# Position bias tables of the sparse attention made at the program's start, one row per head, through a DRAM table

## What is computed

```
def rel_bucket(dist):
    n = jnp.maximum(dist, 0)
    ...
    return jnp.where(n < max_exact, n, large)
...
    table = rel_bias.astype(f32).reshape(REL_BUCKETS, G, HPG).transpose(1, 2, 0)
...
        lc = (jnp.einsum('bghqd,bgkd->bghqk', qc, k_cmp).astype(f32) * scale
              + table[:, :, rel_bucket(tq[:, None] - cmp_end[None, :])])
...
        lw = (jnp.einsum('bghqd,bgkd->bghqk', qc, kw).astype(f32) * scale
              + table[:, :, rel_bucket(dist)])
```

## Time and profile before

| | before |
|---|---|
| median of 3 runs | 1943.29 us (1943.08 to 1943.59) |
| profiled execution | 1943.08 us, span 1941.3 us |
| TensorE busy | 1815.1 us (94%), mean granted clock 0.959 |
| VectorE, ScalarE, GpSimd busy | 595.7, 358.9, 217.7 us |
| the chain that ended last | TensorE 84%, VectorE 8%, issue 3%, DMA 2% |

### The profile page before, as it was taken

How to read it: one execution, slowest core, us unless ns; L and a number is a source line. 1 busy time by engine, 2 the same in 40 slices (tenths; PEclk the granted TensorE clock), 3 DMA queues, 4 the chain that set the end, 5 groups by cost and what they waited for, 6 DMA issues and landing times.

```text
span 1941.3 us, 25898 instructions
## 1 busy us (share of the span) xinstructions
PE 1815.1 (94%) x11066; PEld 959.5 (49%) x11066; DVE 595.7 (31%) x1273; ACT 358.9 (18%) x842; POOL 217.7 (11%) x263
## 2 busy tenths in 40 slices
PE   7979988989799999999969998999979999999993
PEld 3334347755554454445444576555554444454440
DVE  5463793452221111111040434564122111111113
ACT  1442113311100000000030113665110000000001
POOL 1044000000000000000020001454000000000002
PEclk9989998999799999999969999999979999999997
DMA  5111743060899999999969202010379999999994
GB/s 206 52 78 42 278 123 52 3 268 1 345 414 430 428 427 432 430 428 429 418 233 155 62 22 109 13 30 5 130 289 407 427 432 428 431 427 430 429 402 151
DMA packets 60930, 499.73 MB, mean 257 GB/s; under 512 B 28079, under 2 KB 28591, under 8 KB 42383
## 3 DMA queue, kind: packets, MB, share of 16 engines
q1 hardware_dynamic: 53391, 481.26, 62.1%
q0 software_dynamic: 7424, 16.80, 2.4%
HBM read 465.23 MB, written 41.18 MB: 261 GB/s over the span
## 4 chain that ended last, share of the span: by engine, by line
PE 84%; DVE 8%; issue 3%; DMA 2%; POOL 1%; ACT 1%; SPq 0%; POOLq 0%; DVEq 0%
PE bank L1397 71%; PE bank L1449 5%; PE bank L1985 3%; PE bank L1999 2%; DVE spare L1008 2%; DVE arena L1009 1%; PE bank L1785 1%; DVE arena L1260 1%; DMA arena<-y_rows,ints 1%; POOL arena L493 1%; DMA arena<-gram_dram 1%; PE bank L1405 1%; POOL arena L491 0%; DVE arena L1022 0%; PE bank L1557 0%
## 5 line engine op out<-in xcount | busy, mean ns | idle before, releaser
L1397 PE MATMUL bank<-arena 128*64 128x512 f32 (+10 forms) x5202 | 1258.8, 540 | 25.3 <-DVE arena L973 9.5
L1397 PEld LDWEIGHTS bank<-arena 128*64 128x64 f32 (+5 forms) x5202 | 485.2, 156 | 675.9 <-issue 653.0
L1397 PEld LDWEIGHTS bank<-const,arena 128*128 128x128 f32 x2048 | 238.2, 195 | 51.2 <-issue 48.7
L1397 PE MATMUL bank<-const,arena 128*128 128x128 f32 x2048 | 250.0, 281 | 2.2 <-DVE const L1139 2.2
L513 POOL DMA_INDIRECT y_rows<-arena,ints x64 | 63.0, 985 | 1124.3 <-ACT arena L749 909.5
L1214 DVE TENSOR_TENSOR arena<-arena,bank 128x256 f32<-128x256 f32 x64 | 26.9, 421 | 426.5 <-ACT arena L743 426.5
L749 ACT ACTIVATE arena<-bank 128x512 f32<-128x512 f32 x64 | 38.2, 597 | 424.3 <-PE bank L1397 424.3
L743 ACT ACTIVATE arena<-bank 128x256 f32<-128x256 f32 x64 | 24.5, 383 | 468.6 <-PE bank L1397 468.6
L1146 DVE TENSOR_TENSOR arena<-bank,vec 128x512 f32<-128x512 f32 x64 | 44.3, 691 | 192.7 <-PE bank L1397 192.7
L559 POOL TENSOR_SCALAR arena<-arena,small 128x128 f32<-128x128 f32 (+3 forms) x128 | 76.5, 607 | 150.6 <-DVE small L1374 150.6
L1223 DVE COPY arena<-bank 128x256 f32<-128x256 f32 x64 | 27.1, 424 | 184.3 <-PE bank L1785 184.3
(11 more groups left out here) (238 smaller groups left out, 980.7 us busy)
## 6 DMA issues: line engine op xcount, KB each, us to landing
arena<-m_w SPq DMA_DIRECT2D x64, 4096.0 KB, 18.5
arena<-m_w SPq DMA_DIRECT2D x64, 2048.0 KB, 16.5
y_rows<-state SPq DMA_DIRECT2D x1, 8192.0 KB, 22.6
arena<-kv_w SPq DMA_DIRECT2D x1, 6144.0 KB, 18.3
rev_bias<-arena SPq DMA_DIRECT2D x1, 5120.0 KB, 69.7
arena<-a_wk SPq DMA_DIRECT2D x2, 2048.0 KB, 14.9
arena<-a_wr SPq DMA_DIRECT2D x2, 2048.0 KB, 7.9
arena<-a_wv SPq DMA_DIRECT2D x2, 2048.0 KB, 8.0
```

The source lines that it names most:

```text
L1397: return nc.tensor.matmul(dst, lhsT, rhs, start=start, stop=stop)
```

## The change

It does four things.

- The one-hot matrices and the bias values are loaded once, by ScalarE's own DMA instructions, as its first three instructions. Four products (three of 16x512, one of 16x128) are the first on TensorE. VectorE copies their results into `bias_rows` (16 rows of 1664) ahead of its first normalization step; SP writes them to DRAM behind the first weight loads.
- The columns of `bucket_fwd` are permuted on the way in, so that `bias_c` is eight DMA reads of that DRAM table (rows of 55 values), issued behind the load of `w_kv`.
- `rev_dram` is filled from the DRAM table instead of from SBUF, without a wait of its own.
- The 57 products, the four copies and the six loads at the end of the first mixture of experts go. Several semaphore names share counters in a new way; that moves no instruction.

```diff
+            sp.wait_ge(sem("bias_ev"), 4)
+            sp.dma_start(bias_dram, bias_rows).then_inc(sem("bias_out"), 16)
             sp.wait_ge(sem("tr_done"), NK)
...
             sp.wait_ge(sem("expert_mm"), at("expert_mm", E - 2))
-            for i in range(2):
-                sp.dma_start(fwd[i], d["bucket_fwd"]).then_inc(sem("bias_in"), 16)
-                sp.dma_start(rev[i], d["bucket_rev"]).then_inc(sem("bias_in"), 16)
-                sp.dma_start(rel[i][0:32, :], d["rel_bias"]).then_inc(sem("bias_in"), 16)
...
             sp.dma_start(w_kv, d["kv_w"]).then_inc(sem("kv_w_in"), 16)
+            for a in range(8):
+                sp.dma_start(bias_c[16 * a:16 * a + 16, :, :],
+                             bass.AP(tensor=bias_dram.tensor, offset=9 - a, ap=[[64, 16], [1664, NH], [1, NOFF]])
+                             ).then_inc(sem("bias_c_in"), 16)
...
-            sp.wait_ge(sem("rev_ev"), at("rev_ev", 1))
-            sp.dma_start(rev_dram, spread(rev_rows, 1, P)).then_inc(sem("rev_out"), 16)
+            sp.dma_start(rev_dram, spread(bias_dram[:, 1024:1664], 1, P)).then_inc(sem("rev_out"), 16)
...
+            nc.scalar.dma_start(fwd, d["bucket_fwd"]).then_inc(sem("bucket_in"), 16)
+            nc.scalar.dma_start(rev, d["bucket_rev"]).then_inc(sem("bucket_in"), 16)
+            nc.scalar.dma_start(rel[0:32, :], d["rel_bias"]).then_inc(sem("bucket_in"), 16)
             act.wait_ge(sem("gn_eps"), 1)
...
+            act.wait_ge(sem("bias_out"), 16)
             for m in range(4):
                 k_squares(m)
...
-            act.wait_ge(sem("bias_mm"), at("bias_mm", 1))
-            nc.scalar.activation(rev_rows[:, 0:512], bank[2][0:NH, :], ACT.Copy, scale=-1.0)
-            nc.scalar.activation(rev_rows[:, 512:640], bank[3][0:NH, 0:128], ACT.Copy, scale=-1.0)
...
+            nc.vector.memset(rel[32:33, :], NEG).then_inc(sem("rel_mask"), 1)
+            dve.wait_ge(sem("bias_mm"), 1)
+            for i in range(2):
+                nc.vector.tensor_copy(bias_rows[:, 512 * i:512 * i + 512], bank[4 + i][0:NH, :]).then_inc(sem("bias_ev"), 1)
+            nc.vector.tensor_scalar(bias_rows[:, 1024:1536], bank[6][0:NH, :], -1.0, None, ALU.mult).then_inc(sem("bias_ev"), 1)
+            nc.vector.tensor_scalar(bias_rows[:, 1536:1664], bank[7][0:NH, 0:128], -1.0, None, ALU.mult).then_inc(sem("bias_ev"), 1)
             for j in range(NJ + 1):
...
+            dve.wait_ge(sem("bias_c_in"), at("bias_c_in", 128))
             then(nc.vector.tensor_scalar(cmask, bias_c[:, 0, :], 0.1 * NEG, None, ALU.is_gt))
...
+            pe.wait_ge(sem("bucket_in"), 48)
+            pe.wait_ge(sem("rel_mask"), 1)
+            for i in range(2):
+                mm(bank[4 + i][0:NH, :], rel, fwd[:, 512 * i:512 * i + 512])
+            mm(bank[6][0:NH, :], rel, rev[:, 0:512])
+            mm(bank[7][0:NH, 0:128], rel, rev[:, 512:640]).then_inc(sem("bias_mm"), 1)
...
-            for m in range(NOFF):
-                mm(bank[m % 2][:, 16 * (m // 2):16 * (m // 2) + 16], fwd[m % 2][:, 864 - 16 * m:992 - 16 * m], rel[m % 2])
-            mm(bank[3][0:NH, 0:128], rel[1], rev[1][:, 512:640])
-            mm(bank[2][0:NH, :], rel[0], rev[0][:, 0:512]).then_inc(sem("bias_mm"), 1)
-            pe.wait_ge(sem("rev_ev"), at("rev_ev", 1))
```

More of the change, by code:

```diff
@@ L63 @@
     "gates_ready": ("l_ready", 8), "xTkv_act": ("d_ready", 8), "xTkv_dve": ("e_ready", 8),
-    "router_mm": ("ae_ready", 8), "place_mm": ("r_ready", 8), "b_wo_mm": ("kt_ready", 8), "bias_mm": ("rk_ready", 8),
-    "rel_mask": ("gd_act", 8), "rev_ev": ("gd_masked", 8), "group_shifted": ("lora_mm", 8), "group_exp": ("gd_mm", 8),
+    "router_mm": ("ae_ready", 8), "place_mm": ("r_ready", 8), "b_wo_mm": ("kt_ready", 8),
+    "store_rows": ("rel_mask", 1), "table_zero": ("bias_mm", 1), "table_clear": ("bias_out", 16),
+    "gram_out": ("bucket_in", 48), "tri_in": ("ident_in", 16), "router_in": ("vec_in", 16), "y_clear": ("const_in", 16),
+    "group_shifted": ("lora_mm", 8), "group_exp": ("gd_mm", 8),
     "top_diff": ("g_mm", 8), "top_exp": ("g_ev", 8), "two_hot": ("v_ev", 8), "h_nsa": ("l_kept", 8), "cmp_zero": ("rn_mm", 8),
@@ L268, in decoder_program @@
         bias_c = spare[:, 0:NH * NOFF].rearrange("p (h m) -> p h m", h=NH)
[L269 to L272, removed]
+        fwd, rev, rel = (region(11)[0:33, a:b] for a, b in ((0, 1024), (1024, 1664), (1664, 1680)))
+        bias_rows = region(11)[0:NH, 2048:3712]
+        bias_dram = nc.dram_tensor("bias_rows", (NH, 1664), FP32, kind="Internal").ap()
         xT_b = region(6).rearrange("p (k t) -> p k t", k=NK)
@@ L336, in _ @@
             sp.dma_start(half_w[1], d["a_wv"][1]).then_inc(sem("half_in1"), 16)
-            sp.wait_ge(sem("gram_out"), 256)
+            sp.wait_ge(sem("gram_out"), at("gram_out", 256))
             sp.dma_start(tri, gram_dram).then_inc(sem("tri_in"), 16)
@@ L367, in _ @@
             sp.dma_start(router_b, d["router_b"].rearrange("l p n -> p l n")).then_inc(sem("router_in"), 16)
-            sp.wait_ge(sem("table_zero"), 1)
+            sp.wait_ge(sem("table_zero"), at("table_zero", 1))
             for l in range(2):
@@ L506, in moe_pool @@
             def moe_pool(l):
-                pool.wait_ge(sem("y_clear"), 32)
-                pool.wait_ge(sem("store_rows"), l + 1)
+                pool.wait_ge(sem("y_clear"), at("y_clear", 32))
+                pool.wait_ge(sem("store_rows"), at("store_rows", l + 1))
                 for e in range(E):
@@ L520, in moe_pool @@
                 with pool.If(n_over > 0):
-                    pool.wait_ge(sem("table_clear"), 32)
+                    pool.wait_ge(sem("table_clear"), at("table_clear", 32))
                     for j in range(NJ):
@@ L986, in _ @@
             ring_mix(2, 3)
-            dve.wait_ge(sem("tri_in"), 16)
+            dve.wait_ge(sem("tri_in"), at("tri_in", 16))
             flat = tri.rearrange("p s t -> p (s t)")
@@ L1049, in _ @@
                     if c == 0:
-                        dve.wait_ge(sem("y_clear"), 32)
+                        dve.wait_ge(sem("y_clear"), at("y_clear", 32))
                     for par in range(2):
@@ L1411, in _ @@
                 for k in range(NK):
+                    if j == 0 and k >= 4:
+                        pe.wait_ge(sem("bias_ev"), k - 3)
                     last = nc.tensor.transpose(bank[k][:, P * j:P * j + P], xn[:, j, P * k:P * k + P], ident)
@@ L1743, in moe_pe @@
                 projected(6)
-                pe.wait_ge(sem("router_in"), 32)
+                pe.wait_ge(sem("router_in"), at("router_in", 32))
                 pe.wait_ge(sem(added), at(added, 6))
@@ L2114 @@
     x["consts"], x["bucket_rev"], x["bucket_fwd"] = shape_constants()
+    at = np.arange(1024)
+    x["bucket_fwd"] = x["bucket_fwd"][:, 16 * (63 - at % 64) + at // 64]
     nc = bacc.Bacc("TRN2", target_bir_lowering=False, num_devices=1, dynamic_dma_scratch_size=8192)
```

10 lines of the change are left out of this document (1 added, 9 removed), and 2 rows, old and new, of the table GOES_ON.

## The result

The changed kernel takes 1948.28 us (median of 22 executions, 1943.26 to 1960.95) where the kernel before takes 1942.99 us (22 executions, 1937.57 to 1950.63). The ratio is 1.0032 [1.0022, 1.0043]: slower by 0.32%, and the interval lies wholly above 1. The medians alone are 5.3 us apart (a ratio of 1.0027), and the ratio of 1.0032 stands for 6.2 us. In 4 of the 22 executions of the kernel before and 3 of the 22 of the changed one, the time is 6 to 13 us longer than the median. The profiled execution took 1949.12 us and its span grew from 1941.3 to 1947.2 us, 5.9 us.

The account below looks back on a forecast made before the run. TensorE was busy 94%, but the start's chain of waits was taken to decide: landing 5.0, start 0.1, products 5.2, copies 2.35, step 0.15 put root 0 +4.2 us later; removal and middle 0; 1947.5 us, range 1944.2 to 1950.5.

Parts of the forecast that it names:

- The sum as a whole: At the start, landing, products, copies and normalization step add up; root 0 moves from 8.64 to about 12.85 us, +4.2 us.
- The rival by which less is lost: At the start, earlier landing, full-clock products or warm transposes: 1943.5 to 1947.1 us, taken at 1945.5; 40%.
- Step 1, the landing: Start: ScalarE's three loads land at 5.0 us, using a small early load's 3.4 us landing; bounds 4.1 and 8.9.
- Step 2, the products: Start: four bias products on TensorE take 5.2 us, with 2.9 (full clock) and 5.8 (half clock) as ends.
- Step 3, the copies: Start: VectorE's four copies out of PSUM take 2.35 us, then the first normalization step 0.15 us.
- x's second block: Start: the new loads hold up the second block of x by 0.7 us at most, hidden behind VectorE.
- The transposes and the projection: Behind root 0: transposes start at 14.2 instead of 9.96 us, as slow as before; everything moves by 4.2 us.
- The rival "less is lost" by warm transposes: Part of the 40% rival: products lift the clock, transposes save some 1.5 of 6.3 us, giving +2.7 us.
- a projection at full clock: Part of the 40% rival: the first projection's 5.13 us at half clock run at full clock, saving another 2.6 us.
- The removal: End of first mixture of experts: the 114 removed instructions lie under the gather of the experts' rows; worth 0.
- The middle adds: Middle: eight `bias_c` reads on SP at 0.63 us each delay what follows by 5 us, but are covered; 0.
- The copy from DRAM to DRAM: Middle: as long as before, cost 0; rival at twice the time stalls the second compression MLP, +31 us, 3%.

Follow-up runs that it names:

- first experiment: Changed kernel with VectorE's wait and four copies moved behind its normalization loop and the transposes reordered; 1940.71 us, ratio 0.9989 to the kernel before.
- fourth: Changed kernel with all four products and copies 128 columns wide, most of the bias table left zero; 1943.42 us, ratio 1.0010 to the kernel before.
- fifth: Kernel before with the three new loads on ScalarE's queue at the start, unused; 1941.57 us, ratio 0.9998 to the kernel before.
- second: Kernel before with everything of the change, but done at the old place in the middle; 1943.11 us, ratio 1.0007 to the kernel before.
- third: Changed kernel with the old six loads, 57 products and four ScalarE copies put back, results unused; 1948.40 us, ratio 1.0026 to the kernel before.

## Why the prediction was right, by its own steps

**The sum as a whole.** Forecast 1947.5 us, measured 1948.28. That is nearer than the change itself was forecast: +4.2 us against 5.3 by the medians and 6.2 by the ratio, a fifth to a third too little, while the kernel before came out 0.3 us lower than the median that the forecast started from. The rival by which less is lost had 40% against the forecast's 45%. The mechanism was right: new work ahead of the first normalization step in VectorE's written order delays root 0, and the delay is carried to the end unshortened. The first, fourth and fifth experiments show it: with the work at another place the loss is gone, with a fraction of the work most of it is gone, and the loads by themselves cost nothing. The sum gave +4.2 us and root 0 moved by 5.54, so the forecast was 1.3 us too low at root 0.

**Step 1, the landing.** Forecast 5.0 us; the wait ended at 6.2 and the first product started at 6.25. Too low by 1.2 us, the largest of the three errors. ScalarE's first issue took 0.61 us, and the third went out at 1.69 as forecast; the landing took 4.52 us behind that, not the 3.4 of the row that was chosen, and 4.9 to 5.1 us in the four other runs that wait for it. The row itself did not stay what it was: the same 64 KB load took 4.7 us in the changed kernel. It took 4.5 to 5.0 us in all six runs with the three early loads and 3.4 to 3.6 in all six without them. So the added loads slow a small load beside them by about 1.2 us, which is the size of the miss, and a row of the kernel before was the wrong measure for them. The blocks of x took 5.9 us instead of 6.3. What the loads compete for was not isolated.

**Step 2, the products.** Forecast 5.2 us, with 5.8 as its upper end, and measured 5.72: too low by 0.5 us. All six wide passes took 1052 ns on average, close to the 1044 ns of a pass at half clock; the rise that the forecast let fall inside them did not come. The page's window gives them a granted clock of 1.00, as it gave, and their durations contradict it.

On this the Trainium skill, page "TensorE: Matmul & The Clock Gate", section "What's actually happening", says that the throttled state is the default and that activity ends it; the trace agrees with it by the 1052 ns and the 424 ns, and not with the window's 1.00.

**Step 3, the copies.** Forecast 2.35 us and 0.15 for the step, measured 12.01 to 14.18 us, 2.17 in all. Too high by 0.3 us: copies of one engine follow each other at 0.64 us, not at the 0.69 of a lone one.

**x's second block.** A delay of up to 0.7 us was allowed for; it arrived at 7.11 us instead of 7.58.

**The transposes and the projection.** They move with root 0 (5.55 and 5.67 us) and are as slow as before: the first 26 take 5.79 us, against 5.73 for 27. The clock fell in the gap ahead of the projection as forecast. The windows of the changed kernel at the projection's start and five microseconds on:

```profile
25.00:26.00 1.00, 0.06 (x1) 0.09 (x1) 0.96 (x3) 0.00 (x0) 0.00 (x0) 0.50 1.01 426
...
30.00:31.00 1.00, 1.00 (x2) 0.34 (x1) 0.96 (x2) 0.00 (x0) 0.00 (x0) 0.50 0.00 0
31.00:32.00 1.00, 1.00 (x3) 0.53 (x2) 0.96 (x3) 0.00 (x0) 0.00 (x0) 0.72 0.00 0
```

The half-clock stretch has moved with the work. The rival "less is lost" by warm transposes fell, since the 33-row products did not lift the clock. Its sizes were sound: transposes that wide products precede are 2.1 us shorter than in the trace of before and 1.2 shorter than in that of the loads alone (rival: 1.5), and a projection at full clock is 2.6 and 1.7 us shorter (rival: 2.6).

**The removal.** Forecast 0, and 0 by the second and third experiments. The idle time ahead of the transposes is 18.53 us, the 18.5 forecast to a hundredth or so. A busy share of 94% would have misled here: it hid a wait of 9.19 us on another engine.

**The middle adds.** Forecast 0 with 5 us of SP's time for eight reads; they held SP for 15.08 us, three times as long. The mis-sized term was still hidden: the load of the next weights went out at 1084.39 us, 6.56 later than in the earlier trace rows, which is the shift that everything there has, and L1339 waited for nothing.

**The copy from DRAM to DRAM.** Forecast as long as before, measured 21.8 us instead of 69.7. That rival, given 3%, did not come. The trace of before had no row for this transfer, and "as long as before" was three times too long.

**Open.** The shift grows from 5.67 us at the projection to 6.58 at 1018 us and comes back to 5.9 at the end. No experiment isolates this; the spread between executions is as large (the products' first wait ends anywhere from 6.2 to 6.8 us, and the projection of an unchanged start begins anywhere from 19.01 to 20.76 us).

## What to carry to other kernels

Where engines work through a written order, side work placed ahead of the head of the chain is paid as far as it ends later than what the chain waited for before, however idle the engine looks. Here the products and copies ran for 7.8 us, from 6.25 to 14.08, and root 0, which had started at 8.64, moved by 5.5. Ask what the next instruction behind it is and who waits for that, and put the side work's consumer (here the copies) behind it. Work taken from the busiest engine gives nothing where that engine waits for another one directly afterwards. An idle gap of TensorE ahead of a long run of products can be worth filling with throwaway wide products: here three at the head and three in the gap gave 0.21%, with an interval from 0.10 to 0.32%. And before a difference of a microsecond between two traces is explained, look at a trace in which that part was left alone: here the unchanged start differed by 1.8 us between executions.

## What the runs showed of the hardware

- 5.7 us of products from 33 rows to 16 columns left TensorE at the durations of its lower level, 1.2 GHz (1052 ns a pass), in all four runs that have them. In the first experiment the transposes follow them without a pause, and the first 16 still take 424 ns. Six passes of 128 rows and 128 columns ahead of the transposes took 944 ns on average, and the transposes behind them 278 ns against 349 to 404 with nothing ahead; in the gap ahead of the projection six such passes took 2.58 us in all, 0.43 each, half of the 0.86 that a pass takes at 0.50, so the higher level, 2.4 GHz.
- The granted clock of the first microseconds is 1.00 in the windows of both kernels, while the durations there are those of 0.50 (424 ns a transpose from 10 to 12 us, 1052 ns a pass). Read durations at the start of a trace.
- The copy out of DRAM moved 5 MB in 21.8 us, where the same bytes from 16 partitions took 69.7 us. Part of the 69.7 us is waiting, since 8 MB of weights had been issued 3 us ahead; but with these landed, the window from 1040 to 1060 us of the kernel before shows 100 GB/s, and that from 1038 to 1052 us of the changed one 344. The Trainium skill, page "SBUF — State Buffer", section "Door 1: The DMA port swizzle", says that 16 neighbouring partitions reach four of the 16 ports through which DMA reads SBUF, which it puts at about 109 GB/s; the 100 GB/s of the old copy agree with it, and the new copy does not read SBUF.
- Eight reads with rows of 220 bytes took 15.08 us to issue, 1.9 us each, while a 6 MB load was in flight. The nearest rows of before had 0.63 us. What held them up is not isolated.
